# Emptying a PSUM bank ahead of a weight refill, and two moves in steps 9 and 10 of a transformer kernel

## The reference

```python
def first_block(x, c, ...):                # stages a and b
    h = rmsnorm(x) * (1 + scale) + shift   # scale, shift, gate = c @ w_ada + b_ada
    q_a, k_a, v_a, z_a, q_b, k_b, v_b, z_b, f, g = split(h @ w_in)
    y_a = (stick_breaking(q_a, k_a, v_a) * silu(z_a)) @ w_o_sb      # 8 heads of 64
    y_b = (forgetting_attention(q_b, k_b, v_b, f) * silu(z_b)) @ w_o_fox
    merged = sigmoid(g[0] + b) * y_a + sigmoid(g[1] + b) * y_b
    return rmsnorm(x + gate * (merged @ w_out))

def second_block(x, mem, ...):
    # hybrid mixer: differential attention (4 heads, rotated q and k) beside
    # a causal depthwise convolution of 31 taps over 512 gated channels
    a = diff_attention(rope(q), rope(k), v, lam)
    c = silu(layernorm(dwconv(u[:, :512] * sigmoid(u[:, 512:]), w31) + bias))
    x = x + concat(rmsnorm(a), c) @ w_out_2
    x = x + cross_attention(rmsnorm(x), rmsnorm(mem))     # 256 memory rows
    x = x + conv_ffn(rmsnorm(x))                          # 2816 wide, 3 taps
    return rmsnorm(x)
```

## Time and profile before

| | us |
|---|---|
| median of 3 runs | 1352.53 |
| lowest and highest | 1351.33 to 1352.85 |
| the profiled execution | 1353.44 |
| span of its instructions | 1351.6 |
| PE busy | 1300.7 |
| DVE busy | 752.7 |
| POOL busy | 734.2 |
| ACT busy | 568.7 |
| mean granted clock of PE | 0.982 |

### The profile page before, as it was taken

One profiled execution on the slowest core, in us unless ns is written; L12 is line 12 of the kernel. 1 busy time (PEld: TensorE's weight loads), 2 busy tenths in 40 slices (PEclk: granted clock), 3 DMA queues, 4 the chain that ended last, 5 costly groups with the idle time before them and its releaser, 6 DMA issues.

```text
span 1351.6 us, 17298 instructions
## 1 busy us (share of the span) xinstructions
PE 1300.7 (96%) x6354; PEld 1079.5 (80%) x6354; DVE 752.7 (56%) x1292; ACT 568.7 (42%) x919; POOL 734.2 (54%) x858
## 2 busy tenths in 40 slices
PE   5999999999999999999989899999999999999997
PEld 5778788878788778887767897888888888888885
DVE  5756777434334247498676524665537724651554
ACT  2555565455455335322444555344433423331331
POOL 0643434343333476576342687642738967885782
PEclk9999999999999989999998999999999999999998
DMA  9621224232323642223213344311322332323321
GB/s 330 222 79 39 78 71 141 82 105 71 125 86 115 228 138 79 92 94 94 78 53 119 94 138 141 113 63 32 110 78 92 96 123 92 98 94 96 94 92 62
DMA packets 41701, 142.81 MB, mean 106 GB/s; under 512 B 4625, under 2 KB 5009, under 8 KB 40465
## 3 DMA queue, kind: packets, MB, share of 16 engines
q1 hardware_dynamic: 41616, 141.71, 32.2%
HBM read 131.21 MB, written 8.39 MB: 103 GB/s over the span
## 4 chain that ended last, share of the span: by engine, by line
PE 81%; DVE 11%; ACT 4%; DMA 2%; issue 1%; POOL 1%; DVEq 0%; SPq 0%; ACTq 0%; POOLq 0%
PE ps L135 80%; DVE ac L148 3%; DMA raw<-units 2%; DVE tm L145 2%; ACT tm L142 1%; PE ps L139 1%; DVE x L148 1%; ACT wh L142 1%; ACT L142 1%; DVE tm L148 1%; DVE spl L145 1%; DVE ma L148 0%; DVE sph L156 0%; POOL ycl L145 0%; DVE ewl L145 0%
## 5 line engine op out<-in xcount | busy, mean ns | idle before, releaser
L145 POOL TENSOR_TENSOR wl<-raw,wh 128x256 fp32r<-128x256 f32 x804 | 679.6, 878 | 558.8 <-ACT wh L142 558.5
L142 ACT ACTIVATE wh<-raw 128x1024 fp32r<-128x1024 f32 x201 | 212.5, 1057 | 441.8 <-PE ps L135 431.0
L135 PE MATMUL ps<-hh,wh 128*128 128x512 f32 x872 | 344.6, 395 | 1.3 <-ACT ge L142 1.3
L135 PE MATMUL ps<-hh,wl 128*128 128x512 f32 x872 | 340.5, 390 | 0.0
L135 PE MATMUL ps<-hl,wh 128*128 128x512 f32 x872 | 340.5, 390 | 0.0
L135 PEld LDWEIGHTS ps<-hh,wh 128*128 128x128 f32 x872 | 164.6, 189 | 36.1 <-ACT ge L142 1.7
L135 PEld LDWEIGHTS ps<-hh,wl 128*128 128x128 f32 x872 | 164.2, 188 | 35.0
L135 PEld LDWEIGHTS ps<-hl,wh 128*128 128x128 f32 x872 | 164.5, 189 | 33.1
L148 DVE SCALAR_TENSOR_TENSOR tm<-cb,par_sb,tm 128x512 f32<-128x512 f32 x88 | 87.1, 990 | 50.5 <-ACT tm L142 47.2
L145 DVE TENSOR_TENSOR tm<-tm,tm 128x512 f32<-128x512 f32 (+3 forms) x106 | 90.7, 860 | 39.3 <-ACT tm L142 36.5
L142 ACT ACTIVATE tm<-tm 128x512 f32<-128x512 f32 (+3 forms) x109 | 54.2, 531 | 95.2 <-DVE tm L148 79.2
(11 more groups left out here) (309 smaller groups left out, 2377.7 us busy)
## 6 DMA issues: line engine op xcount, KB each, us to landing
raw<-units SPq DMA_DIRECT2D x217, 512.0 KB, 3.5
kept<-ge SPq DMA_DIRECT2D x16, 256.0 KB, 2.0
tm<-kept SPq DMA_DIRECT2D x16, 256.0 KB, 3.8
tm<-gate_w SPq DMA_DIRECT2D x12, 256.0 KB, 4.0
x<-xin SPq DMA_DIRECT2D x2, 1024.0 KB, 9.6
x<-xin SPq DMA_DIRECT2D x1, 2048.0 KB, 9.8
out<-x SPq DMA_DIRECT2D x8, 256.0 KB, 2.2
kv<-kvt SPq DMA_DIRECT2D x1, 1536.0 KB, 8.5
```

Of the source, the lines that this page charges most:

```text
L135: return self.none if self.e is None else self.e.matmul(out, lhs, rhs, start=start, stop=stop, skip_group_check=skip)
L142: return self.none if self.e is None else self.e.activation(out, in_, func, **kw)
L145: return self.none if self.e is None else self.e.tensor_tensor(out, a, b, op)
```

## The change

1. In ScalarE's `qk_high`, `z_gate`, `gate` and `dproj` the call of `refill` moves from the front to behind the emptying of the bank.
2. In ScalarE's loop over the sixteen steps the emptying of the convolution is a function of its own, `conv_out`, and stands ahead of the refill. At odd steps it comes first, then `turn_d`, and the refills of the convolution's units come behind `turn_d`. The refill for the first unit of keys or values of a step also moves behind `turn_d`.
3. `conv_out(15)`, the emptying of the last convolution block, moves on ScalarE from step 10 to step 9, behind `turn_d(9)` and ahead of `join_d(10)`. The refill for that unit stays in step 10, behind `pv_d(4)`. PE's own piece `conv(15)` keeps its place.
4. On PE in step 10 the transposes `turn_d(10)` come ahead of `kv(0, 0)`, which stood before them.

No instruction is added or removed. DVE, POOL and SP keep their order.

```diff
@@ PE, the sixteen steps
-                if n >= KV_STEP:
+                if n > KV_STEP:
                     kv(n - KV_STEP, 0)
...
             turn_d(n)
             if step in (1, 4):
                 dproj(h, step + 1)
+            if n == KV_STEP:
+                kv(0, 0)
             if n >= KV_STEP:
                 kv(n - KV_STEP, 1)
@@ ScalarE
         def qk_high(br, c, what):
             p = c % 2
-            refill((br + what, c))
...
             act.fn(d[p][:, :], PS[qkz_bank(br, c, what)][:, :], ACT.Copy).then_inc(*s.up(br, c))
+            refill((br + what, c))
 
         def z_gate(br, c):
-            refill((br + "z", c))
...
             act.fn(SZ[c % 2][:, :], PS[qkz_bank(br, c, "z")][:, :], ACT.Silu).then_inc(*s_sz.up(br, c))
+            refill((br + "z", c))
 
         def gate(n):
-            refill(gate_unit(n))
...
                    bias=pcol("b_gate", gate_unit(n)[1])).then_inc(*s_gl.up(n))
+            refill(gate_unit(n))
@@
         def conv(x):
-            j, q = 2 + x // 8, x // 2 % 4
-            if x % 2 == 0:
-                return
-            refill(("cw", j, q))
-            if q == 3:
+            conv_out(x)
+            if x % 2:
+                refill(("cw", 2 + x // 8, x // 2 % 4))
+
+        def conv_out(x):
+
+            j = 2 + x // 8
+            if x % 8 == 7:
                 act.wait_ge(s_unit, ("cw", j, 3))
@@ dproj
-            refill((nm, h))
...
             act.fn(RTh[:, :], PS[b][:, :], ACT.Copy).then_inc(*s_rh.up(nm, h))
+            refill((nm, h))
@@ ScalarE, the sixteen steps
-            if n and n % 2 == 0 and n != KV_STEP:
+            convs = range(cw_done(n), cw_done(n + 1))
+            if n and n % 2 == 0:
                 pv_d(n // 2 - 1)
             if n % 2 == 0:
-                for x in range(cw_done(n), cw_done(n + 1)):
-                    conv(x)
-            if n == KV_STEP:
-                pv_d(n // 2 - 1)
+                for x in convs:
+                    if n == KV_STEP:
+                        refill(("cw", 3, 3))
+                    else:
+                        conv(x)
...
             if n % 2:
-                for x in range(cw_done(n), cw_done(n + 1)):
-                    conv(x)
+                for x in convs:
+                    conv_out(x)
+            turn_d(n)
+            if n % 2:
+                for x in convs:
+                    if x % 2:
+                        refill(("cw", 2 + x // 8, x // 2 % 4))
             if n >= KV_STEP:
                 refill(kv_units(n - KV_STEP)[0])
-            turn_d(n)
+            if n == KV_STEP - 1:
+                conv_out(15)
```

## The result

The changed kernel takes 1332.65 us (median of four runs, 1331.19 to 1337.62), beside it the kernel before 1352.69 (four runs, 1351.33 to 1360.13). The ratio is 0.9847 with an interval of 0.9803 to 0.9891. The forecast was 1339.7 us in a range of 1336.5 to 1347.0: the direction was right, the size was not, and the time lies 4 us under the lower end.

What follows compares the result with a forecast made beforehand. TensorE, busy 1300.7 of 1351.6 us, was taken as the bound, its stalls costing themselves and sometimes clock. Terms 2.25 + 1.8 + 1.7 + 2.85 + 4.2 = 12.8 us gave a median of 1339.7, range 1336.5 to 1347.

Steps and rivals of the forecast that it cites:

- stage b, waits for `ge`: Stage b: emptying ahead of the refill cuts the longest wait to about 0.75 and removes two others, 2.25 us.
- stage a, idle: Stage a: GpSimd's passes start later, so DVE's chain to `kl` runs freer, 1.8 us, with 0.6 us of stall left.
- differential attention to step 9, idle: Projections and odd steps: earlier emptying shortens PE's waits, 1.2 + 0.45 + 0.3 + 0.9 = 2.85 us, between 1.5 and 4.0.
- step 10, idle: Step 10: earlier scores, and the 2.99 us wait for `ac` replaced by about 0.5 for the joined row; 3.4 us without clock.
- clock behind `kl`: Stage a, stretch 170 to 175: the fall to 0.66 of the clock goes with the 1.85 us stall, 1.7 us; bound nothing.
- clock in step 10: Step 10: the 1.75 us fall of the clock may stay or go; the middle was taken, making steps 9 and 10 4.2 us.
- the rest of the clock: All other stretches of the span: the sum held no term for clock lost there.
- growing waits for `dkl`: Sign in the profile after: if waits for `dkl` and `kl` grow instead, GpSimd's passes were the wrong step.
- the 3.2 of the prediction: Sign in step 10: three transposes stand before the first unit of keys, which comes some 3.2 us closer to the scores.
- The direct waits alone: First rival: DVE's chains do not pass their lead on; 5.7 us, 1346.8; chance 0.32 shared with the lead given back.
- No lead was given back in steps 11 to 15: Second rival claimed PE waits there for weights' low parts, losing 4.2 us: 8.6 gained, 1343.9; chance 0.32 shared with direct waits.
- The passes fell off the chain, not on it: Third rival claimed GpSimd's later passes cover DVE's chains, slower by 16 us, 1368; slower had chance 0.04.

Runs made afterwards that it cites:

- The late passes: Kernel before, with only GpSimd's passes of stages a and b also waiting for ScalarE's emptying of the bank; 1348.98 us, ratio 0.9929.
- the nine profiles above: Profiles of the kernel before and its variants with the old order from 600 us to step 10; they lose 4.2 us of clock there on average.
- the repeat: The changed kernel run once more without any edit, on another chip; 1334.09 us (the kernel before, likewise repeated, 1356.89).
- the table above: Clock lost in us, by part of the span, in all profiles of the kernel before, the changed kernel and their variants.
- the five kernels: Unread matmuls ahead of waits: kernel before with `kl` by 4 (1354.0 us), by 8 (1355.12), `ac` (1355.01); changed kernel with opening (1335.65), `dkl` (1334.68).
- eight ahead of `kl`: Kernel before with eight unread matmuls on PE ahead of its wait for `kl` at 168; 1355.12 us, ratio 0.9996.

## Why the prediction was wrong in size

Its steps in order, against the first pair of profiles:

| term | predicted | measured |
|---|---|---|
| stage b, waits for `ge` | 2.25 | 2.20 |
| stage a, idle | 1.8 | 2.66, and 0.92 in the opening |
| differential attention to step 9, idle | 2.85 | 3.06 |
| step 10, idle | 3.35 | 1.50 |
| other idle time | 0 | 0.2 |
| clock behind `kl` | 1.7 | 1.7 |
| clock in step 10 | 0.85 (0 to 1.75) | 0 |
| the rest of the clock | 0 | 9.0 |

- **Stage b** was right: the wait at the end is 0.78 and the other two are gone.
- **Stage a** had the right mechanism and was too small. The late passes leave 0.64 us at `kl`, by their own experiment. I had costed only them, though the same edit also brings `qh` and `kh` forward; together nothing is left. The opening, with waits of 0.55 and 0.75 us that fell to 0.15 and 0.23, was not in my sum at all. The term is 1.8 us short.
- **The differential attention** came out in sum: 1.67 fell to 0.73 as foretold, 0.26 went, 1.03 for `ac` went while the third `dkl` grew from 0.2 to 0.4 and not to 0.8, and the rest gave 1.04 for 1.2.
- **Step 10** went as described, but its idle time moved to another wait. 2.99 for `ac` became 0.51 for the joined row. The wait for `dkl` was to come 0.96 us earlier; it grew from 0.61 to 1.59 instead. The prediction had the condition for it (1.6 us, if 735 to 740 runs at full clock) and yet kept the 0.96 in the sum. It had also named growing waits for `dkl` as a sign against GpSimd's passes; by the nine profiles above this one grew because PE came at full clock. In the first profile of the kernel after the unit of keys in step 10 still ran at half clock for 3.4 us, as before; in the repeat it did not. From these scores to the next the first pair saves 2.5 us (11.57 to 9.09), the repeats 4.0 (11.58 to 7.56). Less the 0.98 us by which the wait for `dkl` grew, that is 1.5 and 3.0, where the forecast had 4.2. The first unit of keys came 1.9 us closer to the scores; the 3.2 of the prediction do not follow from its own starts (741.85 and 743.4), which give 2.3.
- **The clock** is the step that failed. The prediction priced it at the waits that it looked at, 1.7 and 0.85, and set the rest at nothing. In the first pair of profiles the rest is 9.0 us. By stretches it is 1.7 in the opening, 3.4 at 495 to 510, 3.4 from 600 to step 10, 1.7 at 775, less 1.7 at 290: 8.5; the other 0.5 is not placed. By the table above the 3.4 at 495 to 510 are chance, and in their place other falls came or went: the mean cost of the clock over all runs is 23.7 to 26.3 us for the kernel before in four groups of 8 to 25 runs, and 14.3 and 14.0 for the changed one in two of 4. About 10 us of clock are thus no accident of one profile, against 2.55 in the sum. The averages of the table would place 8.4 of them (3.4 + 2.2 + 1.5 + 1.3); of these only the 3.4 stand clear of the spread and have a filled wait beside them.

The Trainium skill (TensorE: Matmul & The Clock Gate, "Part 1: The HAM clock gate") says that the counting is free of the program, and that the slow matmuls at the start of a kernel differ in number from run to run for it. For falls in the middle of a kernel the two repeats show the like: nearly the same waits, other falls, in one case none behind 1.84 us. The prediction used that rule to say that 1.7 us might stay away. By the averages above it cuts both ways: idle time taken away takes with it the chance of a fall that it had in other runs, and not only where the one profile shows a fall.

Of the rivals, none came. The direct waits alone would have been 5.7 us, and idle time alone fell by 10.5. No lead was given back in steps 11 to 15: matmul by matmul it is 20.1 us at 800, and the same at 1300. The passes fell off the chain, not on it. The weight that I gave to over 16 us, 0.03, was the error in the range: its upper end summed the bounds of the idle terms and the two falls that it had priced (1.7 and 1.75 us), with nothing for the rest of the clock.

What stays open: how the clock's gain divides among the places, stage a and 600 to step 10 above all, and what decides whether a given stall is followed by a fall. No version beat the changed kernel by more than can be measured.

## What to carry to other kernels

Before pricing a change that removes stalls of TensorE, sum the clock lost over the whole span, place by place, and give each stall its share: here some 10 us of clock went with 10.5 us of stall. A second profile of the same kernel shows cheaply some of the stretches that are chance, and the mean granted clock of every run, which costs nothing, shows whether a loss is one profile's or the kernel's. Empty a bank before refilling a weight slot where both wait for the same event, and look at who runs under the refill: in stage a the delay of GpSimd's passes alone took 2.0 of the 2.66 us of stall.

## What the runs showed of the hardware

- The same program spreads widely on one chip: 1351.12 to 1363.59 us in 25 runs of the kernel before. The span less the cost of the clock has a standard deviation of 0.9 to 1.5 us in the five groups of runs of this kernel, against 2.2 to 3.5 us for the time, so the spread is mostly the clock's.
- From 45 us on each fall in the 17 profiles lost 1.7, 3.4 or 5.1 us, but for the one at the very end, where PE has no work left.
- A fall ahead of a wait for another engine costs less time than it loses clock: 0.7 of 1.7 us ahead of the scores of step 10, where the wait shrank from 1.59 to 0.6.
- Filling nearly all of a stall with matmuls that nobody reads takes the fall of the clock away in the place itself, but in none of the five kernels that did it did the median fall by more than can be measured: the lead went into the next wait (eight ahead of `kl`), the clock fell elsewhere (the opening, `dkl`), or the 3.0 us won lie within the noise of the median (`ac`).
- A stall of 0.97 us was still followed by a fall in one profile, one of 1.84 was followed by none in another. The length of the stall alone does not decide.
